# A two-layer hybrid decoder step on one core: new order of the first unit of each layer, and rope on GpSimd

## The reference, cut to what matters

```python
def hybrid_layer(x, C0, n0, m0, S0, k_buf, v_buf, pos0, norm_gain, w_in, gate_bias, ...):
    u = rms_norm(x, norm_gain)
    proj = jnp.einsum('btd,dc->btc', u, w_in).astype(f32)
    (mq, mk, mv, mo, mz, mi, mf, rq, rk, rv, rz, aq, ak, av, az) = jnp.split(proj, split_points, axis=-1)
    h_m, C, n, m = mlstm(heads(mq, M_HEADS), ...)          # 4 heads, gate rows mi, mf
    out_m = head_norm(sigmoid(mo) * h_m, m_gain, M_HEADS) * silu(mz)
    h_r, S = retention(rope(heads(rq, R_HEADS), pos), rope(heads(rk, R_HEADS), pos), ...)
    out_r = head_norm(h_r, r_gain, R_HEADS) * silu(rz)
    h_a, kw, vw = window_attention(heads(aq, A_HEADS), ..., sinks, rel_table)
    out_a = h_a * silu(az)
    mix = concatenate([out_m, out_r, out_a])
    return x + jnp.einsum('btc,cd->btd', mix, w_out), ...
```

## Time and profile before

| | |
|---|---|
| median of 3 runs | 2201.43 (2201.23 to 2204.5) |
| profiled execution | 2199.84, span 2198.0 |
| TensorE busy | 2091.5 (95%), 13170 matmuls |
| DVE busy | 1597.2 (73%) |
| ACT busy | 864.6 (39%) |
| GpSimd busy | 316.2 (14%) |
| granted TensorE clock, mean | 0.975 of 2.4 GHz |

### The profile page before, as it was taken

How to read it: one execution, slowest core, us unless ns; L and a number is a source line. 1 busy time by engine, 2 the same in 40 slices (tenths; PEclk the granted TensorE clock), 3 DMA queues, 4 the chain that set the end, 5 groups by cost and what they waited for, 6 DMA issues and landing times.

```text
span 2198.0 us, 37141 instructions
## 1 busy us (share of the span) xinstructions
PE 2091.5 (95%) x13170; PEld 1186.9 (54%) x13170; DVE 1597.2 (73%) x3856; ACT 864.6 (39%) x2298; POOL 316.2 (14%) x342
## 2 busy tenths in 40 slices
PE   3899999999999999999979999999999999999997
PEld 2555555655555565444545555555565556554443
DVE  6867777777777777666465777777777777778856
ACT  5834344444444445331145444444444434462100
POOL 1011111111111111120000111111111111111200
PEclk8899999999999999999989999999999999999989
DMA  9210000000000003594541000000000001136632
GB/s 291 68 30 21 20 20 35 25 20 20 20 20 20 21 20 106 142 241 132 160 156 60 25 21 20 20 20 20 21 20 20 20 22 38 30 124 176 165 102 91
DMA packets 133506, 143.27 MB, mean 65 GB/s; under 512 B 93079, under 2 KB 107096, under 8 KB 133276
## 3 DMA queue, kind: packets, MB, share of 16 engines
q1 hardware_dynamic: 116116, 110.08, 17.5%
q0 software_dynamic: 7424, 29.43, 3.7%
q10 hardware_dynamic: 9896, 2.84, 0.6%
HBM read 85.35 MB, written 42.29 MB: 58 GB/s over the span
## 4 chain that ended last, share of the span: by engine, by line
PE 78%; DVE 13%; ACT 3%; issue 3%; DMA 1%; SPq 0%; ACTq 0%; POOL 0%; DVEq 0%; POOLq 0%
PE J L527 49%; PE J L1193 11%; PE W L895 3%; PE W L915 3%; PE T L868 1%; PE W L905 1%; DVE uT_mix L1623 1%; DVE W L520 1%; ACT W L513 1%; PE W L975 1%; PE J L950 1%; PE W L1004 1%; PE W L995 1%; DVE ST L1730 1%; ACT uT_mix L1239 1%
## 5 line engine op out<-in xcount | busy, mean ns | idle before, releaser
L527 PE MATMUL J<-W,uT_mix 128*128 128x512 f16 (+2 forms) x6144 | 1222.7, 356 | 21.4 <-DVE W L520 8.4
L527 PEld LDWEIGHTS J<-W,uT_mix 128*128 128x128 f16 x6144 | 599.1, 99 | 570.2 <-issue 27.8
L1325 ACT ACTIVATE PB<-J,out_scale 128x512 f32<-128x512 f32 (+2 forms) x256 | 154.8, 605 | 308.5 <-PE J L527 304.5
L1193 PE MATMUL J<-W,EM_qkR_mix 128*128 128x512 f16 x480 | 117.0, 383 | 0.0
L1295 ACT ACTIVATE ST<-ST,small 128x1024 f16<-128x1024 f32 x32 | 36.8, 1149 | 173.2 <-DVE small L1746 173.2
L1193 PE MATMUL J<-W,uT_mix 128*128 128x512 f16 x400 | 100.9, 392 | 0.0
L1660 DVE TENSOR_TENSOR ge<-ge,gr 128x512 f32<-128x512 f32 (+1 forms) x96 | 57.4, 598 | 59.4 <-ACT gr L1262 59.3
L1290 ACT ACTIVATE sc_xr<-sc_xr,small 128x128 f32<-128x128 f32 x256 | 98.6, 389 | 0.0
L1193 PE MATMUL J<-W,x_mix 128*128 128x512 f16 x400 | 96.1, 379 | 0.0
L1239 ACT ACTIVATE uT_mix<-T 128x512 f16<-128x512 f32 x64 | 34.7, 594 | 130.5 <-PE J L527 120.1
L1623 DVE SCALAR_TENSOR_TENSOR uT_mix<-T,uT_mix 128x512 f16<-128x512 f32 x64 | 41.2, 685 | 61.2 <-ACT uT_mix L1239 59.3
(11 more groups left out here) (443 smaller groups left out, 3464.0 us busy)
## 6 DMA issues: line engine op xcount, KB each, us to landing
W<-in_w_in POOLq DMA_DIRECT2D x8, 2048.0 KB, 13.7
mix_d<-ST SPq DMA_DIRECT2D x32, 512.0 KB, 2.8
x_mix<-in_x_prompt SPq DMA_DIRECT2D x16, 512.0 KB, 3.6
ST<-in_w_in POOLq DMA_DIRECT2D x4, 2048.0 KB, 14.6
W<-in_w_out SPq DMA_DIRECT2D x4, 2048.0 KB, 7.7
x_mix<-x SPq DMA_DIRECT2D x16, 512.0 KB, 3.8
PB<-in_x_prompt SPq DMA_DIRECT2D x6, 512.0 KB, 3.5
x<-PB SPq DMA_DIRECT2D x6, 512.0 KB, 3.8
```

Of the source, the lines that this page charges most:

```text
L527: mm = nc.tensor.matmul(out, stationary(k, a), moving[:, k, b, :], start=(k == 0 and n == 0), stop=(k == KT - 1 and n == 2))
L1193: mm = nc.tensor.matmul(J[n], of_tile[:, s, k, :], w[:, cols], start=(k == 0 and i == 0), stop=(k == KT - 1 and i == 2))
L1325: return af(dst, src, ACT.Copy, scale=scale)
```

## The change

In layer 0 the sample rows are loaded third on SP, their norm moves ahead of the first block's maximum, and their transposes ahead of the first product. The second block's sizing leaves the start; in both layers sizes, scales, splits, products and evacuations of blocks 0 to 5 follow each other in a new order, the banks of some products change, and the gate rows' steps, `tokens`, `em` and `spread_rows` move among them. In layer 0 the load of the next chunk waits for the first sample keep, the store of the Toeplitz rows moves behind the fifth, and ACT waits for it ahead of `m_gate_exp`. In both layers rope and scaled keys go from DVE to GpSimd (`first_rope`), behind the load of `mvo`; DVE waits for the rope ahead of `gate_cap`. Of the queues that are reordered the new lines are shown, with "..." where lines are removed; the old ones stand in the functions above.

```diff
@@ -673,16 +673,18 @@
         def start_sp(sp):
             sp.dma_start(x, A["x_prompt"][0][0:CHUNK, :]).then_inc(E["x_loaded"], 16)
             load_gain(sp, 0)
+            sp.dma_start(xs, A["x_sample"].rearrange("b t d -> (b t) d")).then_inc(S["x"], 16)
             sp.dma_start(ident, A["c128"][:, 0:P]).then_inc(ident_loaded, 16)
             sp.dma_start(k4[:], A["c4"]).then_inc(ident_loaded, 16)
             sp.wait_ge(E["cleared"], 1)
             sp.dma_start(tab[0:N_BUCKETS, :], A["rel_bias_table"]).then_inc(table_loaded, 16)
             sp.dma_start(oneh, A["onehot"]).then_inc(table_loaded, 16)
-            sp.dma_start(xs, A["x_sample"].rearrange("b t d -> (b t) d")).then_inc(S["x"], 16)
             sp.wait_ge(w_loaded["rqk"], 16)
             sp.dma_start(ropet[:], A["rope"][0:CHUNK, :]).then_inc(E["rope_loaded"], 16)
             load_layer(sp, 0)
             sp.dma_start(k128[:, P:N128], A["c128"][:, P:N128]).then_inc(const_loaded, 16)
+
+        def store_toeplitz(sp):
             sp.wait_ge(toep_sb, 1)
             sp.dma_start(bass.AP(toep, 0, [[P * TOEP, A_HEADS], [TOEP, P], [1, TOEP]]),
                          gt.unsqueeze(1).to_broadcast([A_HEADS, P, TOEP])).then_inc(toep_stored, 16)
@@ -730,9 +732,12 @@
 
             for i in range(RING):
                 wait(sp, o_stored[i], 16 * layer * SLOT_TILES[i])
-            next_x(N0, 0)
             for p in range(NBLK):
                 keep_sample(p)
+                if p == 0:
+                    next_x(N0, 0)
+                if layer == 0 and p == 4:
+                    store_toeplitz(sp)
             next_rope(N0, 0)
 
             def unit(n, c, attn, more):
@@ -1023,39 +1026,60 @@
             n, P0, S0 = N0, NBLK * N0, NBLK * layer
             pe.wait_ge(E["uT_ready"], n + 1)
             wait(pe, Q["y_added"], 2 * TILES * layer)
...
+
+            def sample_turn():
+                pe.wait_ge(*seen("u", layer))
+                for k in range(KT):
+                    mm = TR(T[1][:, k * TS:(k + 1) * TS], xs[:, k * P:(k + 1) * P], ident[0:TS, 0:TS])
+                mm.then_inc(raised("xT_psum"), 1)
+
             if layer == 0:
+                sample_turn()
+                first_block(0, 0)
+                top_turn(pe, layer, 1)
+                top_spread(pe, layer, 1)
+                pe.wait_ge(*seen("uT", layer))
+                sample_block(0, 1)
+                top_turn(pe, layer, 2)
+                pe.wait_ge(E["proj_evac"], P0 + 1)
+                rows_turn(n)
+                top_spread(pe, layer, 2)
+                first_block(1, 0)
                 top_turn(pe, layer, 3)
...
+                pe.wait_ge(s_evac, S0 + 1)
+                sample_block(1, 1)
+                top_spread(pe, layer, 3)
+                pe.wait_ge(E["proj_evac"], P0 + 2)
+                first_block(2, 0)
+                top_turn(pe, layer, 4)
+                pe.wait_ge(s_evac, S0 + 2)
+                sample_block(2, 1)
+                top_spread(pe, layer, 4)
+            else:
+                first_block(0, 0)
+                top_turn(pe, layer, 4)
+                first_block(1, 1)
+                top_spread(pe, layer, 4)
+                sample_turn()
+                pe.wait_ge(E["proj_evac"], P0 + 1)
+                rows_turn(n)
+                first_block(2, 0)
+                pe.wait_ge(*seen("uT", layer))
+                pe.wait_ge(E["proj_evac"], P0 + 2)
+                sample_block(0, 1)
+                pe.wait_ge(E["proj_evac"], P0 + 3)
+                sample_block(1, 0)
                 top_turn(pe, layer, 5)
...
+                pe.wait_ge(s_evac, S0 + 1)
+                sample_block(2, 1)
+                top_spread(pe, layer, 5)
+                pe.wait_ge(s_evac, S0 + 2)
             pe.wait_ge(const_loaded, 16)
...
             for p in range(3, NBLK):
                 pe.wait_ge(E["proj_evac"], P0 + p)
                 first_block(p, 0)
                 if p == 3:
+                    spread_rows(n)
                     r_turn(n)
                 if layer == 0 and p < 6:
                     top_turn(pe, layer, p + 2)
@@ -1208,10 +1232,9 @@
                 name=nc.get_next_instruction_name(), engine=mybir.EngineType.Activation,
                 act_func_set_id=EXP_LN_SET, ins=[], outs=[]))
             prompt_rstd(act, 0)
+            sample_rstd(act, 0)
             block_sum(act, 0, 0)
             prompt_uT_hi(act, 0)
-            sample_rstd(act, 0)
-            block_sum(act, 0, 1)
 
         def load_bias(act):
 
@@ -1385,47 +1408,54 @@
                 cp(qkR, B[0]).then_inc(E["rqk_ready"], 1)
 
             n, P0 = N0, NBLK * N0
+
+            def sample_uT_hi():
+                act.wait_ge(*seen("xT_psum", layer))
+                af(uTs[:, 0].rearrange("p k t -> p (k t)"), T[1], ACT.Copy, scale=U_SCALE).then_inc(raised("uT_hi"), 1)
+
             if layer == 0:
                 block_hi(act, layer, 0)
+                sample_uT_hi()
+                block_sum(act, layer, 1)
+                block_sum(act, layer, 2)
+                evac_first(0, 0)
+                block_hi(act, layer, 1)
+                evac_sample(0, 1)
+                block_sum(act, layer, 3)
                 act.wait_ge(toep_psum, 1)
                 cp(gt, B[0][0:A_HEADS, 0:TOEP]).then_inc(toep_sb, 1)
...
                 block_hi(act, layer, 2)
+                block_sum(act, layer, 4)
+                evac_first(1, 0)
+                evac_sample(1, 1)
+                block_hi(act, layer, 3)
+                evac_first(2, 0)
+                rows_log(n)
+                block_sum(act, layer, 5)
+                rows_exp(n)
+                evac_sample(2, 1)
+                block_hi(act, layer, 4)
             else:
                 act.wait_ge(S["stored"], SAMPLE_STORES * layer)
                 act.wait_ge(prompt_stored, 16 * 9 * layer)
                 sample_rstd(act, layer)
                 block_hi(act, layer, 3)
+                evac_first(0, 0)
+                sample_uT_hi()
+                evac_first(1, 1)
                 block_sum(act, layer, 5)
...
+                rows_log(n)
+                evac_first(2, 0)
+                rows_exp(n)
+                evac_sample(0, 1)
+                evac_sample(1, 0)
                 block_hi(act, layer, 4)
...
+                evac_sample(2, 1)
                 block_hi(act, layer, 5)
             evac_first(3, 0)
             r_gate_exp(n, P0 + 4)
             r_keys(n)
+            em(n)
             block_sum(act, layer, 6)
             evac_sample(3, 1)
             gate_log(n, "r")
@@ -1448,6 +1478,8 @@
             m_keys(n)
             prompt_rstd(act, n + 1)
             evac_first(7, 0)
+            if layer == 0:
+                act.wait_ge(toep_stored, 16)
             m_gate_exp(n, P0 + NBLK)
             gate_log(n, "m")
             gate_first(n, "m")
@@ -1578,13 +1610,11 @@
             clear_states(dve)
             prompt_norm(dve, 0)
             gain_size(dve, 0)
+            sample_norm(dve, 0, xs)
             block_max(dve, 0, 0)
             top_of_all(dve, 0, 0)
             prompt_uT_lo(dve, 0)
-            sample_norm(dve, 0, xs)
             block_scale(dve, 0, 0)
-            block_max(dve, 0, 1)
-            top_of_all(dve, 0, 1)
 
         def clear_states(dve):
             V = nc.vector
@@ -1872,51 +1902,58 @@
                                 ).then_inc(E["wR_ready"], 1)
 
             n, P0 = N0, NBLK * N0
+
+            def sample_uT_lo():
+                dve.wait_ge(*seen("uT_hi", layer))
+                V.scalar_tensor_tensor(uTs[:, 1].rearrange("p k t -> p (k t)"), T[1], U_SCALE,
+                                       uTs[:, 0].rearrange("p k t -> p (k t)"), ALU.mult, ALU.subtract
+                                       ).then_inc(raised("uT"), 1)
+
             if layer == 0:
                 block_lo(dve, layer, 0)
+                sample_uT_lo()
+                block_max(dve, layer, 1)
+                top_of_all(dve, layer, 1)
                 block_scale(dve, layer, 1)
                 block_max(dve, layer, 2)
+                block_lo(dve, layer, 1)
                 top_of_all(dve, layer, 2)
...
+                block_scale(dve, layer, 2)
                 block_max(dve, layer, 3)
...
                 block_lo(dve, layer, 2)
...
+                top_of_all(dve, layer, 3)
+                block_max(dve, layer, 4)
                 block_scale(dve, layer, 3)
                 block_lo(dve, layer, 3)
                 top_of_all(dve, layer, 4)
+                dve.wait_ge(layer_loaded, 16 * LAYER_DMAS * (layer + 1))
+                dve.wait_ge(const_loaded, 16)
+                rows_in(n)
+                block_scale(dve, layer, 4)
                 block_max(dve, layer, 5)
...
+                rows_scan(n)
+                rows_out(n)
+                block_lo(dve, layer, 4)
+                tokens(n)
+            else:
+                block_scale(dve, layer, 3)
+                top_of_all(dve, layer, 4)
```

(35 more changed lines are left out.)

84 lines of the change are left out of this document (removed).

## The result

The kernel after takes 2210.56 us (median, 2207.36 to 2213.51), beside 2200.68 for the kernel before on the same chips: a ratio of 1.0045, 95% interval 1.0031 to 1.0059. It is slower, by 9.9 us, where I forecast 2199.1 in 2194 to 2207.

What follows compares the result with a forecast made beforehand. TensorE held 78% of the chain; the change touches each layer's first unit. Layer 0's -7.6 and layer 1's +5.3 give -2.3, from 2199.84 to 2197.5; the median lying 1.6 higher, 2199.1 us, range 2194 to 2207.

Steps and rivals of the forecast that it cites:

- the term for the store's drain: Layer 0, Toeplitz store on SP: takes 20 us, lands at 108 to 110 before `m_gate_exp`; cost 0, bounds 0 and 14.
- Rival (1): Layer 0's store drains in 36 us even alone, `m_gate_exp` starts 5.7 later: 2212.4 us; chance 0.15.
- Layer 0's order: New order of layer 0's first unit: `block_hi(6)` 8.75 us earlier, 7.6 after the GpSimd cost.
- the marker: Start of `block_hi(6)`, followed in each layer: 95.45 before in layer 0, 1177.21 before in layer 1.
- the 1.1 for GpSimd: Layer 0, DVE steps waiting beside GpSimd's rope: 1.1 us lost, bounds 0 and 3.
- the walk: Step-by-step layer 0 estimate: fourth product at 54, `block_hi(4)` 63.5, `block_hi(5)` 76.2, `block_hi(6)` 86.7.
- the sample norm: Start of layer 0 on DVE, ahead of the first maximum: cost taken as 0, or 0.8 if the load still takes 8.5.
- GpSimd's rope in layer 0: Rope and scaled keys on GpSimd from 44.1 to 49.1, long before `r_turn` at 64.6, relieving DVE of 2.6 us.
- Layer 1: GpSimd's rope waits behind the `mvo` load, delaying `r_turn`: `block_hi(6)` 5.3 us later, bounds 3.9 and 7.
- Rival (2): The rope does not hold layer 1, `block_hi(6)` comes 4.2 earlier there: 2189.6 us; chance 0.10.

Runs made afterwards that it cites:

- runs 13 and 14: Changed kernel, Toeplitz store still from 8 partitions, but 4 apart (2195.9 us) or 16 apart (2195.6 us) instead of neighbouring.
- Run 7: Changed kernel with store through memory (128 outermost), layer 1's rope ahead of the `mvo` load, and sample rows loaded fifth on SP: 2185.9 us.
- run 3: Changed kernel with GpSimd's rope and scaled keys ahead of the load of `mvo` in layer 1: 2200.2 us.
- run 11: Changed kernel with store from 128 partitions, placed ahead of the sample stores, and layer 1's rope ahead of the `mvo` load: 2185.1 us.
- run 12: Kernel before with only its Toeplitz store changed, read from 128 partitions at its old place: 2201.1 us, ratio 0.9997.
- run 8: Changed kernel with the slow store behind the sample block's third stores instead of the fifth: 2201.9 us, ratio 1.0010.
- run 1: Changed kernel with the Toeplitz store put back ahead of the sample block's stores on SP: 2209.0 us, ratio 1.0040.

## Why the prediction was wrong

**The step that failed** is the term for the store's drain: "alone on the same 8 engines half, 18 ... With 2 for start and receipt I take 20". It measured 36.4, alone, in two kernels. I read two queues at 26% each as engines that take turns, and inferred that without the other queue the store would go twice as fast. But the store's queue moved 0.23 MB in 5 us beside the weights, and 47 to 49 GB/s, which is 0.24 MB in 5 us, alone. The share said how busy the engines were with it, not that another queue held it back. What held it was where its rows stand in SBUF (runs 13 and 14), with the other queue there or not. Rival (1) had the mechanism, the place and the condition, 36 us alone, and gave 2212.4; measured 2210.6. I gave it 0.15, with a reason against it that shares can't bear. Its evidence, an SP load held for 17.79 us, I also read to fit.

**Layer 0's order** was right and 2.0 too good at the marker (87.8 with the 1.1 for GpSimd, measured 89.78). Set beside the walk without that 1.1, the steps come late by nearly the same from the fourth product on: 57.26 for 54, `block_hi(4)` 66.73 for 63.5, `block_hi(5)` 79.37 for 76.2, the marker 89.78 for 86.7. Of these 3.1 to 3.3, 1.3 lie at the start, 0.6 in the second product (7.49 us for 6.91) and 0.9 in the step beside GpSimd, named below; the rest I didn't trace. At the start I let the sample norm cost 0 with a bound of 0.8. The rows of VectorE in the kernel after:

```profile
10.79 0.69 DVE L1663 BATCH_NORM_STATS2 small_n<-sc_xr 64x6 f32<-64x512 f32 x1 [2.27 <-DMA sc_xr<-in_x_sample]
...
14.64 0.96 DVE L452 TENSOR_REDUCE wmax<-W 128x3 f32<-128x792 f32 x1
15.63 0.17 DVE L455 TENSOR_TENSOR wmax<-wmax,gabs 128x8 f32<-128x8 f32 x1
15.84 0.16 DVE L456 TENSOR_REDUCE wtop<-wmax 128x1 f32<-128x8 f32 x1
```

The load landed 9.0 us after its issue at 1.67, though it stood third and not seventh (8.5 there), and the norm took 3.85, so the top is out 1.3 late, at 15.84 where that of before stood at 14.53. Run 7 moves the landing by 1.2 and the top with it.

**GpSimd's rope in layer 0** went as said, 2 us later: 46.20 to 50.99 with the scaled keys (44.1 to 49.1 forecast), long before its user, with one VectorE step stretched beside it.

```profile
49.18 1.14 DVE L504 TENSOR_SCALAR gs<-norm_g,wm 128x8 f32<-128x8 f32 x1
```

It takes 1.14 us instead of 0.23, beside the rope's last addition (49.03, 1.27 us). I had allowed 1.1 in all; this one step costs 0.9. The Trainium skill's rule of a port that one of the two engines holds for a whole instruction (SBUF — State Buffer, SBUF: two separate sides) fits: 1.14 is what was left of the 1.27, 1.12, plus a little.

**Layer 1** was right in mechanism: the load ahead of the rope (1165.30), `r_turn` at 1162.3 in the frame of before (1164.0 forecast), TensorE idle 13.59 (13.7), the marker 4.0 later (5.3). What I didn't follow is the second unit's first product, which ran 1.7 longer at the lower granted clock; why the clock fell there is open. Rival (2), that the rope doesn't hold layer 1, was the right picture of another kernel, run 3: I saw "no path" to it and there was one of three moved lines.

**The number of engines and the ports.** That the outermost dimension of 8 confines a transfer to 8 engines (the Trainium skill, DMA: Bandwidth & Descriptors, Why a DMA increments its semaphore by 16 and not by 1) agrees with the engines' shares: 4 to 5 tenths with 8 outermost, 9 with 128. It told the number of engines and nothing of the rate, and the rate was set elsewhere: by the map of ports named under runs 13 and 14, partitions 0 to 7 have two, which is what 48 GB/s showed. I had not weighed it, though the row with 0.23 MB in 5 us was in front of me.

**The sum as measured**: `m_gate_exp` could start 7.4 earlier (111.2 for 118.61) and waits 15.25, which leaves layer 0 7.6 late at the next product; layer 1 adds 5.5. With 36.4 in the place of 20, my own walk comes out on this side too, as rival (1) says. Without the store's wait the other terms stood near the forecast: 7.4 earlier in layer 0 (7.6) and 5.5 later in layer 1 (5.3). In part that is luck. Layer 0's marker was only 5.7 earlier, and 1.7 came behind it, where the product of block 6 took 5.35 us and not the 7.04 of before; layer 1's marker was 4.0 later, and 1.7 came with the product that I didn't follow.

## What to carry to other kernels

A transfer's drain alone can't be had from its share of the engines while others run, since a full way out of SBUF keeps engines busy as well: divide its bytes by the rate at which its own queue moved, and take that as its own until a run shows it alone. Moving a long transfer on a queue can move the wait from one user of the queue to another, as at all three places tried here. Make it short first, here by reading from partitions that don't share a port; its place then stopped mattering at the two places tried. On an engine with a strict order, look for each moved operation at what it is placed behind: the same rope cost 4 us behind a load that waits and gained 5 ahead of it.

## What the runs showed of the hardware

A store that reads SBUF partitions 0 to 7 moves 48 GB/s, 36.4 us for 1.6 MB, with half of the DMA engines shown as busy; the same bytes from 8 partitions 16 apart take 19 (99 to 107 GB/s), from 8 partitions 4 apart 10.5 (about 195), and from all 128 on 16 engines 5.9 (384). Beside the weight loads the last of these took 12.3 us (run 11) and 17.9 (run 12) to land. The busy share of the engines, 4 to 5 tenths, is the same in the first two: it doesn't tell a waiting engine from a working one. Of each pair of sample stores issued behind the slow one on the same queue, the first landed after 7.2 us in the kernel after and 7.0 in run 8, and the second only about as the slow store ended, 29.8 and 26.3 us after its issue, though 4 to 5 tenths of the engines' time is all that the view shows as busy there. In run 1, beside the weight loads, the pair took 16.5 and 29.6.
